# Six small changes of order in the two mixer layers and the second FFN of a fused transformer kernel on one Trainium2 core

## Chip, core, metric

The kernel runs on one core of one Trainium2 chip. Its engines are TensorE (PE in the profile: matmuls and transposes into PSUM), VectorE (DVE), ScalarE (ACT), GpSimd (POOL) and SyncE (SP, which issues the weight loads). Each engine executes its own list of instructions in order, and the lists meet only at semaphores. The metric is the device time of one execution in microseconds (us), lower is better; a comparison is made by the median of several runs.

## What is computed

The input is one sequence of 256 tokens of width 1024 in float32. Three blocks follow one another. The first has gated linear attention, sliding-window attention and a SwiGLU FFN ("f1"). The second and the third ("layer 0" and "layer 1") each mix with a latent attention and a gated recurrence (HGRN2), side by side:

```
proj = h @ w_in[l]          # split into c_q, c_kv, k_pe, hq, hf, hi, hg
q  = rmsnorm(c_q) @ w_q_b   ;  kv = rmsnorm(c_kv) @ w_kv_b        # "latents" c
a  = causal softmax attention of q against (k_nope, k_pe), 4 heads
f  = lb + (1 - lb) * sigmoid(hf);  k = (1 - lb) * sigmoid(-hf)    # lb: bounds of the layer
S_t = diag(f_t) S_{t-1} + k_t (x) hi_t ;  o_t = S_t^T silu(hq_t)
r  = rmsnorm(o) * silu(hg)
x  = x + concat(a, r) @ w_out[l]
```

The bounds `lb` come from a softmax over the two layers of `hg_lower_bounds`: zero in layer 0, one share per feature in layer 1. Layer 0 is followed by a SwiGLU FFN of inner width 2816 ("f2"), layer 1 by a mixture of 8 experts (top 2), and a last norm ends it.

## The kernel before

**Products.** Every float32 weight piece (128 partitions by 1024 values, two k-tiles of a 512-wide product) is split into a high part, rounded to fp32r, and a low part, the rest. ScalarE makes the high part (line 1542, `split_to`), and then GpSimd (line 669) or, inside the FFNs and the experts, VectorE (lines 2011, 1999) makes the low part by a subtract. TensorE forms three passes (lines 740 to 742): high by high, high by low, low by high. Four buffers hold pieces, so ScalarE may be four pieces ahead of TensorE (semaphore `w_used`). Products of 512 columns end in one of four "gemm banks" of PSUM, numbered by jobs (`gemm_at`); an engine that empties one counts `gemm_read`, and job j waits until job j-4 was read. The other four banks ("pair banks") take transposes and small products in the order of `pair_plan()`; TensorE counts `pair_full`, the reader `pair_read`, and a group waits until the bank's last user was read.

**Order.** Nothing is scheduled by a program: what each engine does and when is the order in which its block lists it. In TensorE's list (`gemm(..., between={...})`) small groups are put between the pieces of a large product.

**The mixers**, lines 1140 to 1290 (TensorE), 1720 to 1815 (ScalarE), 2375 to 2580 (VectorE). For the recurrence the 128 tokens of a tile are halved seven times ("levels", half sizes 64 to 1). Level n needs four steps of VectorE and two of ScalarE: `level_diff(n)` (lines 2439 and 2441, differences of summed log decays for keys and queries), `level_exp(n)` (1755, 1759), `level_scale(n)` (2450), TensorE's `level(n)` (1182, four head products), and `level_take(n)` (2464, masked copy into `n_at`). Level 0 is the diagonal. Other names that matter:

- `turn_gate` (1155 to 1165): waits for `n_lf_ready` (log decays) and forms their sums (1159), then for `n_k_ready` (log keys), transposes these (874), and forms the tails (1164).
- In layer 1, VectorE makes both (2394 to 2405): from `n_tmp[0]` (absolute value, then ScalarE's exponential, `z_odds`) `share` (2396), its product with `bound_rest`, two steps to `f_ready` (2399, 2400), `n_k` (2401), after ScalarE's logarithm `f_log` (1739) `n_lf` (2403), and with `log_rest` (ScalarE, 1735) the last of `n_k` (2405).
- `turn_c` transposes the latents `n_c` when `normalize_c` on VectorE (2493) is done; its factor is made on ScalarE by a logarithm and an exponential (1779, 1780), after the sums of squares (1774).
- `head_gemm` (836, 842): products of the latents with `qb0`, `qb1`, `kvb0`, `kvb1`.
- `hst` (1207): the state after the first tile, copied to `n_st` by VectorE in `copy_out` (1950). `mpT` (1216, 1220): rotated parts of queries and keys, transposed, copied by VectorE and read by the scores `msc0`, `msc1` (1232, 1236).
- `ho` (1247, 1250): output of the recurrence, copied by VectorE to `n_o`; ScalarE squares it (1804) for the norm. `mP` (1261): probabilities transposed; `mo` (1269): attention's output. `mixT` (1282): both transposed for `wo`, which starts in `first_mixed` (808).

TensorE's list from `hi` on is

```
gemm(hi, between={0: level(3), 2: turn_c})
qb0; level(4); qb1; kvb0; level(5); kvb1; hst; mpT; level(6); msc0; level(7); msc1; ho; mP; mo; mixT
```

and VectorE's, from taking level 3 on

```
take(3); cT copies; rotate k; scale(4); diff(5); gains; take(4); scale(5); diff(6); rotate q;
scale(6); take(5); diff(7); copy hst; copy mpT x2; scale(7); take(6); scores ...; copy ho x2; copy mP x3
```

**The FFN** "f2" runs in 11 units of 256 inner columns (`ffn`, lines 2296 to 2350 on VectorE; TensorE 1101 and 1104, `into_both`: all high products of a piece, then the low ones, which wait for VectorE's low half). Ahead of unit 3, VectorE does `finish_bounds()` (2288 to 2294): sum, reciprocal, product and one 1-wide step for layer 1's bounds.

Of the kernel before, what the change touches and what calls it, by code (L numbers as in the profile page):

```python
# [28 lines left out]
ALU = mybir.AluOpType  # L29
# [143 lines left out]
def pair_plan():  # L173

    plan = [("gT", 1), ("hT_f0", 4), ("z", 4), ("gb", 4), ("tail", 2), ("gkT", 2), ("gqT", 2), ("sT", 5),
            ("gsc", 4), ("ssc0", 4), ("gst", 4), ("ssc1", 4), ("go", 4), ("sP0", 4), ("sP1", 4), ("so", 4),
            ("posT", 1), ("soT", 4), ("goT", 4), ("mT", 4), ("hT_f1", 4), ("row_f1", 1)]
    for layer in range(2):
        level = [(f"hlev{n}_{layer}", 1 if n else T) for n in range(len(LEVELS) + 1)]
        plan += [(f"hT_l{layer}", 4), (f"msT_{layer}", 1), (f"hb_{layer}", 2), (f"hkT_{layer}", 2), (f"ht_{layer}", 1),  # L180
                 (f"hqT_{layer}", 2), *level[0:4], (f"cT_{layer}", 3), *level[4:6], (f"hst_{layer}", 1),
                 (f"mpT_{layer}", 2), level[6], (f"msc0_{layer}", 2),
                 level[7], (f"msc1_{layer}", 2), (f"ho_{layer}", 2), (f"mP_{layer}", 3), (f"mo_{layer}", 2),
                 (f"mixT_{layer}", 4),
                 (f"hT_g{layer}", 4)]
        if layer == 0:
            plan += [("row_g0", 1)]
    plan += [("router", 1), ("ranks", 1), ("counts", 1)]
    return plan


def build(nc, A, out):
    gemm_at, jobs = {}, 0
    for name, _, _, width, _ in gemm_plan():
# [78 lines left out]
    with ExitStack() as ctx:  # L273
# [463 lines left out]
        def _(pe):  # L737
# [410 lines left out]
            for l in range(2):  # L1148
# [45 lines left out]
                gemm(f"hi_{l}", between={0: lambda: level(3), 2: turn_c})  # L1194
# [9 lines left out]
                pe.wait_ge(sem("n_kt_ready"), l + 1)  # L1204
                b = pair(f"hst_{l}", 0)
                for i in range(HG_HEADS):
                    mm = pe.matmul(b[:, i * P:(i + 1) * P], n_kt[:, i * P:(i + 1) * P], n_v[:, 0, i * P:(i + 1) * P],
                                   start=True, stop=True)
                mm.then_inc(sem("pair_full"), 1)
# [33 lines left out]
                for t in range(T):  # L1243
                    b = pair(f"ho_{l}", t)
# [7 lines left out]
                    mm.then_inc(sem("pair_full"), 1)  # L1252
# [211 lines left out]
        def _(act):  # L1464
# [257 lines left out]
            for l in range(2):  # L1722
# [11 lines left out]
                if l == 1:  # L1734
                    act.activation(log_rest, bound_rest, ACT.Ln, bias=least_rest).then_inc(sem("rest_log"), 1)
# [36 lines left out]
                for t in range(T):  # L1772
# [6 lines left out]
                link(act.activation(head_rinv[:, 8:12], head_ms[:, 8:12], ACT.Ln))  # L1779
                act.activation(head_rinv[:, 8:12], head_rinv[:, 8:12], ACT.Exp, scale=-0.5) \  # L1780
                    .then_inc(sem("c_rinv"), 1)
# [18 lines left out]
                act.wait_ge(sem("pair_read"), pair_end[f"ho_{l}"])  # L1800
# [7 lines left out]
                act.activation(head_rinv[:, 0:8], head_ms[:, 0:8], ACT.Sqrt).then_inc(sem(f"head_root_{l}"), 1)  # L1808
                act.wait_ge(sem(f"head_root_{l}"), told(f"head_root_{l}"))
# [124 lines left out]
        def _(dve):  # L1934
# [353 lines left out]
            def finish_bounds():  # L2288

                dve.wait_ge(sem("bounds_exp"), 1)  # L2290
                link(dve.tensor_tensor(bound_sum, bound_rest, bound_low, ALU.add))
                link(dve.reciprocal(bound_sum, bound_sum))
                mul(bounds, bounds, over(bound_sum, 1, 2))
                link(dve.tensor_scalar(least_rest, ident[:, 0:1], 0.0, LEAST_REST, ALU.mult, ALU.add))
# [79 lines left out]
            for l in range(2):  # L2374
# [109 lines left out]
                def normalize_c():  # L2484
# [12 lines left out]
                def gate_hgrn():  # L2497

                    dve.wait_ge(sem(f"head_root_{l}"), 1)
# [20 lines left out]
                level_scale(3)  # L2520
                level_take(2)
# [12 lines left out]
                level_take(4)  # L2534
                level_scale(5)
# [6 lines left out]
                copy_out(f"hst_{l}", 0, n_st)  # L2542
# [19 lines left out]
                for t in range(T):  # L2562
                    copy_out(f"ho_{l}", t, n_o[:, t, :])

# [217 lines left out]
```

## Time and profile before

| | us |
|---|---|
| median of 3 runs | 1884.51 (1883.92 to 1885.49) |
| the profiled execution | 1884.52, its span 1882.6 |
| TensorE busy | 1859.7 (99%) |
| VectorE busy | 1520.7 (81%) |
| ScalarE busy | 1240.1 (66%) |
| GpSimd busy | 402.8 (21%) |
| chain that ended last | PE 90%, DVE 7%, ACT 1%, issue 1%, DMA 1% |

The span is the time from the first to the last instruction. In rows of the order of time, the first number is the start in us from the span's start, the second the duration (of x instructions together), and brackets hold the idle time before and what ended it. In rows of busy time by stretch, the columns are the stretch, its length, the busy time of PE, PEld (weight loads), DVE, ACT and POOL with their instructions, the granted clock of TensorE (1.00 is 2.4 GHz), the share of the DMA engines and GB/s. Layer 0's mixer lies at 455 to 600 us, the FFN f2 at 600 to 780, layer 1's mixer at 780 to 920, the experts after that. Matmuls are pipelined: a group's duration has a tail of about 0.2 us that the next group overlaps.

### The profile page before, as it was taken

Reading aid. Unit: us, or ns where it says so; the run is one execution under the profiler, and the core shown is the slowest. Engines: PE = TensorE matmul, PEld = TensorE weight load, DVE = VectorE, ACT = ScalarE, POOL = GpSimd, SP = SyncE. Lnnn points to the kernel's source line nnn. Section 1 sums busy time; section 2 is a strip of 40 time slices with the busy share of each in tenths; the row PEclk is TensorE's granted clock in tenths of the full one; section 3 lists DMA queues with packets and bytes.
Section 4 is the critical chain, followed back from the end, with each engine's and each line's share of the span. In section 5 each row is a group of like instructions: output and inputs, shape, how many; then the busy total and the mean of one; then the engine's idle time right before and its main releaser. Section 6 shows DMA issues by size and latency. Waiting matters only on the chain.

```text
span 1882.6 us, 26088 instructions
## 1 busy us (share of the span) xinstructions
PE 1859.7 (99%) x9336; PEld 1563.7 (83%) x9336; DVE 1520.7 (81%) x1650; ACT 1240.1 (66%) x1484; POOL 402.8 (21%) x206
## 2 busy tenths in 40 slices
PE   9999999999999999999999999999999999999997
PEld 7888889888888888878888888888888888888886
DVE  6745357777776887697699999999999999999997
ACT  6654444444754344565588888888888888888876
POOL 6856870002734000371630000000000000000000
PEclk9999999999999999999999999999999999999999
DMA  9534556665444666534699999999999999999994
GB/s 287 169 123 135 179 179 226 223 232 179 132 138 134 218 238 224 163 125 146 221 381 396 391 383 376 388 395 366 388 367 390 395 364 389 366 387 395 371 396 184
DMA packets 251542, 524.20 MB, mean 278 GB/s; under 512 B 9960, under 2 KB 58736, under 8 KB 251328
## 3 DMA queue, kind: packets, MB, share of 16 engines
q1 hardware_dynamic: 243408, 504.00, 74.7%
q10 hardware_dynamic: 5824, 12.06, 1.8%
q0 software_dynamic: 2224, 7.01, 1.2%
q8 instruction: 51, 0.84, 0.2%
q14 instruction: 35, 0.29, 0.0%
HBM read 507.71 MB, written 15.34 MB: 278 GB/s over the span
## 4 chain that ended last, share of the span: by engine, by line
PE 90%; DVE 7%; ACT 1%; issue 1%; DMA 1%; POOL 0%; SPq 0%; DVEq 0%; ACTq 0%
PE bank L740 24%; PE bank L742 24%; PE bank L741 24%; PE bank L1101 6%; PE bank L1104 3%; PE bank L863 1%; PE bank L1368 1%; PE bank L836 1%; DVE arena L1950 1%; DVE arena L2441 1%; DVE arena L1954 1%; PE bank L1182 1%; DMA arena<-in_w_in 1%; DVE arena L2106 1%; PE bank L842 0%
## 5 line engine op out<-in xcount | busy, mean ns | idle before, releaser
L1999 DVE TENSOR_TENSOR w_lo_sb<-arena,w_hi_sb 128x1024 fp32r<-128x1024 f32 x672 | 807.7, 1223 | 74.0 <-ACT w_hi_sb L1522 43.8
L1522 ACT ACTIVATE w_hi_sb<-arena 128x1024 fp32r<-128x1024 f32 x672 | 711.2, 1062 | 168.6 <-PE bank L742 167.9
L740 PE MATMUL bank<-w_hi_sb,left_sb 128*128 128x512 f32 (+1 forms) x1400 | 553.2, 395 | 1.4 <-POOL w_lo_sb L669 1.3
L742 PE MATMUL bank<-w_hi_sb,left_sb 128*128 128x512 f32 (+1 forms) x1400 | 542.2, 387 | 0.0
L741 PE MATMUL bank<-w_lo_sb,left_sb 128*128 128x512 f32 (+1 forms) x1400 | 541.5, 387 | 0.0
L1542 ACT ACTIVATE w_hi_sb<-arena 128x1024 fp32r<-128x1024 f32 (+1 forms) x269 | 278.2, 1051 | 300.8 <-PE bank L742 218.6
L669 POOL TENSOR_TENSOR w_lo_sb<-arena,w_hi_sb 128x1024 fp32r<-128x1024 f32 (+1 forms) x134 | 341.1, 2564 | 536.9 <-ACT w_hi_sb L1542 473.9
L740 PEld LDWEIGHTS bank<-w_hi_sb,left_sb 128*128 128x128 f32 x1400 | 263.1, 188 | 57.9 <-POOL w_lo_sb L669 3.5
L742 PEld LDWEIGHTS bank<-w_hi_sb,left_sb 128*128 128x128 f32 x1400 | 262.9, 188 | 54.9
L741 PEld LDWEIGHTS bank<-w_lo_sb,left_sb 128*128 128x128 f32 x1400 | 263.4, 188 | 50.9 <-issue 0.7
L740 PE MATMUL bank<-w_hi_sb,hid_hi_sb 128*128 128x512 f32 x656 | 257.3, 392 | 0.1
L741 PE MATMUL bank<-w_lo_sb,hid_hi_sb 128*128 128x512 f32 x656 | 255.6, 390 | 0.0
L742 PE MATMUL bank<-w_hi_sb,hid_lo_sb 128*128 128x512 f32 x656 | 255.4, 389 | 0.0
L2011 DVE TENSOR_TENSOR w_lo_sb<-arena,w_hi_sb 128x1024 fp32r<-128x1024 f32 x135 | 160.3, 1217 | 77.6 <-ACT w_hi_sb L1542 76.6
L724 POOL DMA_INDIRECT h_sb<-returned,arena x2 | 2.7, 1366 | 819.7 <-DMA returned<-arena 819.4
L742 PEld LDWEIGHTS bank<-w_hi_sb,hid_lo_sb 128*128 128x128 f32 x656 | 123.1, 188 | 25.9
L740 PEld LDWEIGHTS bank<-w_hi_sb,hid_hi_sb 128*128 128x128 f32 x656 | 123.3, 188 | 25.0 <-DVE w_lo_sb L1999 0.5
L741 PEld LDWEIGHTS bank<-w_lo_sb,hid_hi_sb 128*128 128x128 f32 x656 | 123.3, 188 | 24.2
L1101 PE MATMUL bank<-left_sb,w_hi_sb 128*128 128x512 f32 x512 | 127.8, 391 | 0.0
L1101 PEld LDWEIGHTS bank<-left_sb,w_hi_sb 128*128 128x128 f32 x512 | 93.1, 189 | 17.3
L1954 DVE TENSOR_TENSOR arena<-arena 128x512 f32<-128x512 f32 (+3 forms) x71 | 63.5, 894 | 23.1 <-ACT arena L1553 20.9
L1104 PEld LDWEIGHTS bank<-left_sb,w_lo_sb 128*128 128x128 f32 x512 | 69.8, 190 | 6.4 <-DVE w_lo_sb L2011 1.4
(365 smaller groups left out, 1676.1 us busy)
## 6 DMA issues: line engine op xcount, KB each, us to landing
arena<-in_moe_w_gate SPq DMA_DIRECT2D x112, 1024.0 KB, 7.6
arena<-in_moe_w_up SPq DMA_DIRECT2D x112, 1024.0 KB, 8.0
arena<-in_moe_w_down SPq DMA_DIRECT2D x112, 1024.0 KB, 7.8
arena<-in_w_in SPq DMA_DIRECT2D x45, 1024.0 KB, 5.1
arena<-in_w_ffn_in SPq DMA_DIRECT2D x22, 1024.0 KB, 5.1
arena<-in_w_out SPq DMA_DIRECT2D x12, 1024.0 KB, 5.0
arena<-in_w_ffn_out SPq DMA_DIRECT2D x11, 1024.0 KB, 4.8
arena<-in_dense_w_gate SPq DMA_DIRECT2D x11, 1024.0 KB, 5.4
```

Source lines behind the costliest of these rows:

```text
L669: pool.tensor_tensor(buffer(w_lo_sb, j, k, n), w, buffer(w_hi_sb, j, k, n).bitcast(F32), ALU.subtract).then_inc(sem("w_lo_by_gpsimd"), 1)
L740: pe.matmul(out, still[0], moving[0], start=start, stop=False)
L741: pe.matmul(out, still[0], moving[1], start=False, stop=False)
L742: return pe.matmul(out, still[1], moving[0], start=False, stop=stop)
L836: pe.matmul(gemm_bank[turned % 4][:, j * TOKENS:(j + 1) * TOKENS], w[:, k, j, 0:NOPE], n_cT[:, first + k, :], start=(k == 0), stop=(k == k ...
L1101: pe.matmul(sums, w_hi[:, k, :], left_both[:, :, k, :], start=(k == 0), stop=False)
L1104: mm = pe.matmul(sums[:, 0, :], w_lo[:, k, :], left_hi[:, k, :], start=False, stop=(k == KD - 1))
L1522: act.activation(expert_buffer(w_hi_sb, j), expert_piece(j % MOE_SUBS), ACT.Copy) \
L1542: act.activation(buffer(w_hi_sb, j, *w.shape[1:]), w, ACT.Copy).then_inc(sem("w_hi_ready"), 1)
L1954: dve.tensor_tensor(dst, one, two, ALU.mult).then_inc(sem(name), 1)
L1999: dve.tensor_tensor(expert_buffer(w_lo_sb, j), expert_piece(j % MOE_SUBS), expert_buffer(w_hi_sb, j).bitcast(F32), ALU.subtract) \
L2011: dve.tensor_tensor(buffer(w_lo_sb, j, *w.shape[1:]), w, buffer(w_hi_sb, j, *w.shape[1:]).bitcast(F32), ALU.subtract) \
```

## The change

Six edits, all in lists of order except that two make a factor in another way and one moves copies to another engine.

1. `finish_bounds(step)` is spread over units 3 to 6: sum and the 1-wide step, two halves of the reciprocal, the product.
2. In layer 1 ScalarE makes `log_rest` right after the norm's factor, before three weight casts; VectorE subtracts it from max(z, 0) as the first of its steps, and adds `soft` before `n_lf`.
3. TensorE does `level(3)` after the second piece of `hi` instead of after the first.
4. TensorE makes `hst` after `kvb0`, ahead of `level(5)`; VectorE copies it after `level_take(4)`, ahead of `level_scale(5)`; ahead of the `mpT` copies it waits for `level_diff(7)`.
5. The mean of the latents' squares is made before `level_take(2)`; ScalarE takes one square root and VectorE its reciprocal.
6. `ho` goes into gemm banks (two new jobs after `kvb1`); ScalarE copies it to `n_o`; VectorE's two copies go.

```
 pair_plan:
-    *level[0:4], (f"cT_{layer}", 3), *level[4:6], (f"hst_{layer}", 1), (f"mpT_{layer}", 2), level[6], ...
-    level[7], (f"msc1_{layer}", 2), (f"ho_{layer}", 2), (f"mP_{layer}", 3), (f"mo_{layer}", 2),
+    *level[0:4], (f"cT_{layer}", 3), level[4], (f"hst_{layer}", 1), level[5], (f"mpT_{layer}", 2), level[6], ...
+    level[7], (f"msc1_{layer}", 2), (f"mP_{layer}", 3), (f"mo_{layer}", 2),
 build:
+        if name.startswith("kvb1"):
+            gemm_at[name.replace("kvb1", "ho")], jobs = jobs, jobs + T
 TensorE:
-                gemm(f"hi_{l}", between={0: lambda: level(3), 2: turn_c})
+                gemm(f"hi_{l}", between={1: lambda: level(3), 2: turn_c})
...
                     head_gemm(f"kvb{i}_{l}", Q_RANK // P)
                     if i == 0:
+                        pe.wait_ge(sem("n_kt_ready"), l + 1)
+                        b = pair(f"hst_{l}", 0)
+                        (four head matmuls, then_inc pair_full)
                         level(5)
-                (the same five lines, after the loop)
...
                 for t in range(T):
-                    b = pair(f"ho_{l}", t)
+                    job = gemm_at[f"ho_{l}"] + t
+                    pe.wait_ge(sem("gemm_read"), job - 3)
+                    b = gemm_bank[job % 4]
...
-                    mm.then_inc(sem("pair_full"), 1)
+                    mm.then_inc(sem("ho_full"), 1)
 ScalarE:
                 if l == 0:
                     (bounds exponential)
+                else:
+                    act.activation(log_rest, bound_rest, ACT.Ln, bias=least_rest).then_inc(sem("rest_log"), 1)
                 split_to(span[f"hf_{l}"][1] + BUFFERS + 1)
                 (z_odds, z_soft)
-                if l == 1:
-                    act.activation(log_rest, bound_rest, ACT.Ln, bias=least_rest).then_inc(sem("rest_log"), 1)
...
-                link(act.activation(head_rinv[:, 8:12], head_ms[:, 8:12], ACT.Ln))
-                act.activation(head_rinv[:, 8:12], head_rinv[:, 8:12], ACT.Exp, scale=-0.5) \
-                    .then_inc(sem("c_rinv"), 1)
+                act.activation(head_rinv[:, 8:12], head_ms[:, 8:12], ACT.Sqrt).then_inc(sem("c_rinv"), 1)
...
-                act.wait_ge(sem("pair_read"), pair_end[f"ho_{l}"])
+                for t in range(T):
+                    act.wait_ge(sem("ho_full"), l * T + t + 1)
+                    act.activation(n_o[:, t, :], gemm_bank[(gemm_at[f"ho_{l}"] + t) % 4][:, :], ACT.Copy) \
+                        .then_inc(sem("gemm_read"), 1)
+                act.wait_ge(sem("gemm_read"), gemm_at[f"ho_{l}"] + T)
 VectorE:
+            def finish_bounds(step):
+                if step == 0:
+                    dve.wait_ge(sem("bounds_exp"), 1)
+                    link(dve.tensor_tensor(bound_sum, bound_rest, bound_low, ALU.add))
+                    link(dve.tensor_scalar(least_rest, ident[:, 0:1], 0.0, LEAST_REST, ALU.mult, ALU.add))
+                elif step <= 2:
+                    part = bound_sum[:, (step - 1) * 256:step * 256]
+                    link(dve.reciprocal(part, part))
+                else:
+                    mul(bounds, bounds, over(bound_sum, 1, 2))
...
-                    if tag == "f2" and u == 3:
-                        finish_bounds()
+                    if tag == "f2" and 3 <= u < 7:
+                        finish_bounds(u - 3)
...
                     odds, share = tiles(n_tmp[0]), tiles(n_tmp[2])
+                    dve.wait_ge(sem("rest_log"), 1)
+                    link(dve.scalar_tensor_tensor(n_k, n_z, 0.0, over(log_rest, 1, T), ALU.max, ALU.subtract))
                     dve.wait_ge(sem("z_odds"), 2)
                     (share, odds, then_inc f_ready)
-                    link(dve.scalar_tensor_tensor(n_k, n_z, 0.0, soft, ALU.max, ALU.add))
+                    dve.tensor_tensor(n_k, n_k, soft, ALU.add).then_inc(sem("n_k_ready"), 1)
                     dve.wait_ge(sem("f_log"), 1)
                     dve.tensor_tensor(n_lf, odds, soft, ALU.subtract).then_inc(sem("n_lf_ready_1"), 1)
-                    dve.wait_ge(sem("rest_log"), 1)
-                    dve.tensor_tensor(n_k, n_k, over(log_rest, 1, T), ALU.subtract).then_inc(sem("n_k_ready"), 1)
+                    dve.wait_ge(sem("n_k_ready"), 2)
...
+                def mean_c():
                     (the two means, out of normalize_c)
                 def normalize_c():
                     dve.wait_ge(sem("c_rinv"), l + 1)
+                    link(dve.reciprocal(head_rinv[:, 8:12], head_rinv[:, 8:12]))
...
                 level_scale(3)
+                mean_c()
                 level_take(2)
...
                 level_take(4)
+                copy_out(f"hst_{l}", 0, n_st)
                 level_scale(5)
...
                 level_diff(7)
-                copy_out(f"hst_{l}", 0, n_st)
+                dve.wait_ge(sem(f"level_diff_{l}"), 2 * len(LEVELS))
                 copy_out(f"mpT_{l}", 0, ...)
...
-                for t in range(T):
-                    copy_out(f"ho_{l}", t, n_o[:, t, :])
```

## Rows read from the trace of the kernel before

**Rows 1.** The page, part 1: busy time and share of the span by engine.

```profile
PE 1859.7 (99%) x9336; PEld 1563.7 (83%) x9336; DVE 1520.7 (81%) x1650; ACT 1240.1 (66%) x1484; POOL 402.8 (21%) x206
```

**Rows 2.** Order of time of TensorE, unit 3 of FFN f2.

```profile
647.05 1.22 PE L1104 MATMUL bank<-left_sb,w_lo_sb 128*128 128x256 f32 x8 [1.03 <-DVE w_lo_sb L2011]
```

**Rows 3.** Order of time of VectorE, unit 3 of FFN f2.

```profile
640.21 0.69 DVE L2291 TENSOR_TENSOR arena<-const_sb 128x512 f32<-128x512 f32 x1
640.94 3.35 DVE L2292 RECIPROCAL arena<-arena 128x512 f32<-128x512 f32 x1
...
645.77 4.63 DVE L2011 TENSOR_TENSOR w_lo_sb<-arena,w_hi_sb 128x1024 fp32r<-128x1024 f32 x4
```

**Rows 4.** Order of time of TensorE, layer 1's mixer.

```profile
809.29 2.05 PE L1159 MATMUL bank<-const_sb,arena 128*128 128x128 f32 x16 [0.45 <-DVE arena L2403]
812.61 1.09 PE L874 MATMUL bank<-const_sb,arena 128*128 128x128 f32 x8 [1.26 <-DVE arena L2405]
...
844.66 1.16 PE L1182 MATMUL bank<-arena 128*128 128x128 f32 x8 [1.16 <-DVE arena L2450]
```

**Rows 5.** Order of time of ScalarE, VectorE and GpSimd, start of layer 1's mixer.

```profile
790.62 1.06 ACT L1542 ACTIVATE w_hi_sb<-arena 128x1024 fp32r<-128x1024 f32 x1 [0.30 <-DVE small_sb L2032]
...
798.75 1.28 ACT L1733 ACT_TABLE_LOAD   x1
...
801.02 0.71 ACT L1735 ACTIVATE arena<-const_sb,small_sb 128x512 f32<-128x512 f32 x1
...
794.04 1.23 DVE L1966 SCALAR_TENSOR_TENSOR arena<-arena 128x1024 f32<-128x1024 f32 x1
798.85 2.12 DVE L2396 SCALAR_TENSOR_TENSOR arena<-arena 128x1024 f32<-128x1024 f32 x1 [3.58 <-ACT arena L1731]
...
803.52 3.29 DVE L2400 TENSOR_TENSOR arena<-arena 128x1024 f32<-128x1024 f32 x1
...
791.76 5.76 POOL L669 TENSOR_TENSOR w_lo_sb<-arena,w_hi_sb 128x1024 fp32r<-128x1024 f32 x2 [1.40 <-ACT w_hi_sb L1542]
794.11 3.41 POOL L669 TENSOR_TENSOR w_lo_sb<-arena,w_hi_sb 128x1024 fp32r<-128x1024 f32 x1
...
802.75 2.98 POOL L669 TENSOR_TENSOR w_lo_sb<-arena,w_hi_sb 128x1024 fp32r<-128x1024 f32 x1 [2.86 <-ACT w_hi_sb L1542]
```

**Rows 6.** Order of time of TensorE, middle of the mixers, last row layer 1.

```profile
544.66 1.05 PE L1182 MATMUL bank<-arena 128*128 128x128 f32 x8
545.55 1.89 PE L836 MATMUL bank<-arena 128*128 128x256 f32 x8
...
549.01 1.05 PE L1207 MATMUL bank<-arena 128*128 128x128 f32 x8
...
552.47 1.16 PE L1232 MATMUL bank<-arena 128*128 128x128 f32 x8 [0.86 <-DVE arena L1950]
...
875.23 1.16 PE L1232 MATMUL bank<-arena 128*128 128x128 f32 x8 [0.86 <-DVE arena L1950]
```

**Rows 7.** Busy time of each engine in a stretch; order of time of VectorE there.

```profile
538.91:552.43 13.52, 12.70 (x80) 11.55 (x78) 9.91 (x19) 6.20 (x11) 0.00 (x0) 1.00 0.73 261
...
542.37 1.08 DVE L1954 TENSOR_TENSOR arena<-arena,more_sb 128x256 f32<-128x256 f32 x3 [1.42 <-ACT arena L1562]
...
547.22 0.69 DVE L2450 TENSOR_TENSOR arena<-arena 128x512 f32<-128x512 f32 x1 [1.75 <-ACT arena L1759]
```

**Rows 8.** Order of time of VectorE, TensorE, ScalarE, end of layer 0's mixer.

```profile
560.94 3.58 DVE L1950 COPY arena<-bank 128x512 f32<-128x512 f32 x5
...
563.21 2.92 PE L1269 MATMUL bank<-arena 128*128 128x128 f32 x24 [0.36 <-DVE arena L1950]
...
564.44 0.29 ACT L1804 ACTIVATE arena<-arena 128x128 f32<-128x128 f32 x1
```

**Rows 9.** Busy time of each engine in two slices after the last matmul.

```profile
1875.00:1876.00 1.00, 0.00 (x0) 0.00 (x0) 0.74 (x2) 0.70 (x2) 0.00 (x0) 0.69 0.06 16
1876.00:1877.00 1.00, 0.00 (x0) 0.00 (x0) 0.71 (x1) 0.57 (x1) 0.00 (x0) 0.50 0.00 0
```

More of the change, by code:

```diff
@@ L180, in pair_plan @@
         plan += [(f"hT_l{layer}", 4), (f"msT_{layer}", 1), (f"hb_{layer}", 2), (f"hkT_{layer}", 2), (f"ht_{layer}", 1),
-                 (f"hqT_{layer}", 2), *level[0:4], (f"cT_{layer}", 3), *level[4:6], (f"hst_{layer}", 1),
+                 (f"hqT_{layer}", 2), *level[0:4], (f"cT_{layer}", 3), level[4], (f"hst_{layer}", 1), level[5],
                  (f"mpT_{layer}", 2), level[6], (f"msc0_{layer}", 2),
-                 level[7], (f"msc1_{layer}", 2), (f"ho_{layer}", 2), (f"mP_{layer}", 3), (f"mo_{layer}", 2),
+                 level[7], (f"msc1_{layer}", 2), (f"mP_{layer}", 3), (f"mo_{layer}", 2),
                  (f"mixT_{layer}", 4),
@@ L1202, in _ @@
                     if i == 0:
-                        level(5)
[L1204 to L1208, printed above, removed]
-                mm.then_inc(sem("pair_full"), 1)
+                        pe.wait_ge(sem("n_kt_ready"), l + 1)
+                        b = pair(f"hst_{l}", 0)
+                        for i in range(HG_HEADS):
+                            mm = pe.matmul(b[:, i * P:(i + 1) * P], n_kt[:, i * P:(i + 1) * P], n_v[:, 0, i * P:(i + 1) * P],
+                                           start=True, stop=True)
+                        mm.then_inc(sem("pair_full"), 1)
+                        level(5)
                 pe.wait_ge(sem(f"m_rot_{l}"), 2 * T)
@@ L1251, in _ @@
                                            n_st[:, i * P:(i + 1) * P], start=False, stop=True)
-                    mm.then_inc(sem("pair_full"), 1)
+                    mm.then_inc(sem("ho_full"), 1)
                 for t in range(T):
@@ L1807, in _ @@
                 act.wait_ge(sem(f"head_ms_h{l}"), 1)
-                act.activation(head_rinv[:, 0:8], head_ms[:, 0:8], ACT.Sqrt).then_inc(sem(f"head_root_{l}"), 1)
-                act.wait_ge(sem(f"head_root_{l}"), told(f"head_root_{l}"))
+                act.activation(head_rinv[:, 0:8], head_ms[:, 0:8], ACT.Sqrt).then_inc(sem("head_root"), 1)
+                act.wait_ge(sem("head_root"), told("head_root"))
                 if l == 1:
@@ L2286, in residual @@
                             mean_square("g1")
[L2288 to L2294, printed above, removed]
+            def finish_bounds(step):
[8 more added lines that the diff above has]
+                    mul(bounds, bounds, over(bound_sum, 1, 2))
             def ffn(tag, norm_tag, done, next_tag):
                 for u in range(FFN_UNITS):
-                    if tag == "f2" and u == 3:
-                        finish_bounds()
+                    if tag == "f2" and 3 <= u < 7:
+                        finish_bounds(u - 3)
                     gate_end, up_end = (span[f"{tag}_{kind}{u}"][1] for kind in ("gate", "up"))
@@ L2482, in rotate @@
                         dve.wait_ge(sem(f"m_rot_{l}"), told(f"m_rot_{l}"))
-                def normalize_c():
+                def mean_c():
                     dve.wait_ge(sem(f"c_ss_{l}"), 2 * T)
@@ L2488, in normalize_c @@
                     mean(head_ms[:, 10:12], head_ms[:, 10:12], KV_RANK, "c_ms")
+                def normalize_c():
                     dve.wait_ge(sem("c_rinv"), l + 1)
+                    link(dve.reciprocal(head_rinv[:, 8:12], head_rinv[:, 8:12]))
                     for n, (lo, hi) in enumerate(((0, Q_RANK), (Q_RANK, Q_RANK + KV_RANK))):
@@ L2497, in gate_hgrn @@
                 def gate_hgrn():
-                    dve.wait_ge(sem(f"head_root_{l}"), 1)
+                    dve.wait_ge(sem("head_root"), l + 1)
                     link(dve.reciprocal(head_rinv[:, 0:8], head_rinv[:, 0:8]))
```

## The prediction

> **What bounds the kernel now.** I read the page first: TensorE is busy for 99% of the span, VectorE for 81%, ScalarE for 66% [rows 1]. The time is therefore TensorE's work plus the places where it stands, and an edit counts only where it makes or removes such a place. The second view is TensorE's order of time in the stages that the edits touch. It shows four places where TensorE stands for VectorE: 1.03 us in the fourth unit of the second FFN (unit 3) for a weight piece's low half [rows 2]; in layer 1 0.45 us for the decay logarithms, 1.26 us for the keys `n_k` and 1.16 us for the third level's product [rows 4]; in layer 0 none of the last three. A fifth, 0.86 us ahead of the first scores, stands in layer 0 [rows 6] and likewise in layer 1. The third view is the order of time of VectorE, ScalarE and GpSimd ahead of each such place, for what is late there. After these stages come some 940 us of experts in which TensorE runs without a gap, so what is won or lost before them should reach the end unchanged (slices of the page: TensorE 9 throughout).
>
> The profiled execution took 1884.52 us (span 1882.6, 1.9 around it), and the median of the runs is 1884.51, so sums against the one hold for the other.
>
> **Bounds in four FFN units.** In unit 3 VectorE has 5.56 us of extra work (640.21 to 645.77), of which the 512-wide reciprocal is 3.35 [rows 3]. The low half that follows is ready late by the 1.03 us of TensorE's wait; with the restart after it, start to start, 1.2. So a unit hides 5.56 - 1.2 = 4.4 us of extra VectorE work. After the change the four units get at most: the sum and a 0.15 us scalar step (0.9 together), two halves of the reciprocal (about 1.7 each, half of 3.35), and the 1.23 us product. All lie under 4.4. **-1.2 us** (ends: -1.3 and 0, if another unit had no slack; TensorE has no other wait in the units that are built alike, so I take -1.2).
>
> **Early rest logarithm, layer 1.** ScalarE's `Ln` of 512 (0.71 us [rows 5]) moves ahead of three weight casts, and since the square root stands before it and an exponential after it, a table load of 1.28 us comes with it (such a one is in [rows 5]). The cast at 790.62 then starts about 1.9 us later, at 792.5, and GpSimd's low half of it at 793.6, where it started at 791.76. That matters through VectorE: a VectorE instruction with two operands in SBUF and a GpSimd one do not run side by side. The absolute value of 1.23 us (794.04) made a GpSimd subtract, 2.4 us when alone, last 3.41 us; `share` (L2396) took 2.12, and the sum L2400 3.29 us, beginning while GpSimd was in its piece of 802.75 to 805.73, and each ended about 1.1 us after GpSimd did [rows 5]. Whichever comes first holds the other up whole. So I let them take turns, 2.4 us against 1.1: GpSimd 793.6 to 796.0, absolute value to 797.1; GpSimd to 799.5, the new early `n_k` step to 800.6 (its logarithm has been ready since 792.4, so that wait is none); GpSimd to 803.0, `share` to 804.1; GpSimd (the fourth piece) to 806.5, the product with `bound_rest` to 807.6; then two steps alone to 810.1. Before, L2400 ended at 806.81. ScalarE's logarithm, the rest of `n_k` and `n_lf` follow as before, 2.5 us to TensorE's next group: 812.6 instead of 809.29. The keys are ready by then, so L874 follows L1159's sixteen directly (2.05 us, of which the next group overlaps some 0.2), at 814.4, where it stood at 812.61 [rows 4]. The removed wait of 1.26 comes back as a longer one of nearly 4 us. The other end: if the absolute value gets in ahead of GpSimd as now, L2400 ends where it did and the wait for the keys goes: -1.5 with its restart. +1.8 against -1.5; the row nearest to the new order (absolute value begins at 794.04, GpSimd's new start is 793.6) speaks for the loss; I take **+1.6**.
>
> The Trainium skill says it as a rule (SBUF — State Buffer, section "SBUF: two separate sides"): VectorE with two SBUF inputs and GpSimd take an exclusive lock on a shared port pair, and the later one blocks for the whole instruction. The trace agrees with its 2.12, 3.29 and 3.41 us. If the two shared bandwidth instead, the delay would be about half, and the sum some 1.6 us less.
>
> **Later third level, latents' factor by root.** Level 3 goes one piece of `hi` later, 2.7 us; the wait of 1.16 us in layer 1 [rows 4] is then covered, 1.3 with its restart, as long as VectorE's chain is late by less than that. The factor's chain is two table loads of 1.28 and two small steps (1.5 us each pair); one pair goes, and the mean is made before level 2 is taken, so the latents are normalized some 1.4 us earlier in layer 0, where TensorE did not wait for them: 0 there. The reciprocal adds 0.2 us on VectorE. In layer 1 VectorE is about 2.9 us late after the step above, TensorE 1.6, and the margin is used up: ends -1.5 and 0, I take **-1.3**, layer 1 alone.
>
> **Early state copy.** The diff does two things. TensorE makes the state `hst` after `kvb0` and before level 5. VectorE copies it right after it has taken level 4, ahead of scaling level 5. Times of layer 0: `kvb0` ends and the state can start at 544.66, where level 5 starts now, and the group takes 1.05 us (L1207) [rows 6]: 545.7. VectorE has taken level 4 by 538.9 and would stand for 6.9 us, where it now goes on with scale 5, difference 6, the rotation, scale 6, level 5, difference 7 and three copies. That stretch, 538.91 to 552.43, holds 13.52 us, of which 1.42 and 1.75 us are waits (for ScalarE, in turn for TensorE) [rows 7]: 10.35 us of chain. Begun at 545.8 (a signal costs about 0.1), it ends at 556.15 plus the new wait for difference 7, 0.1. The first scores start at 556.3 instead of 552.47 [rows 6]: **+3.8 us in each layer**; layer 1 has the same form (first scores at 875.23, after the same wait of 0.86). On the way TensorE stands about 1.7 us ahead of level 5 (state copy 0.69, scale 0.69, signals; it is free at 545.55) and about 3 us for the copies of `mpT`, since `kvb1` and the small groups fill only what lies between. What hung on the same VectorE steps moves with them: ScalarE's exponentials 6 and 7 wait for the differences, GpSimd's four pieces for scale 7; all keep their distance. Ends: -0.6 (VectorE is never held and its later copies are one shorter) and +4.0; the nearest rows are the measured chain, so +3.8. Two layers: **+7.6**.
>
> **Recurrent output to ScalarE.** VectorE's five copies of 3.58 us [rows 8] become three. TensorE's L1269 (0.36 us wait for them) can then start when its transposes are done, some 0.57 us earlier; the rest follows. ScalarE copies two banks (about 1.2 us) before its squares, whose last starts at 564.44 now and then at 565.6, while VectorE reads their sum after 566.4: hidden. If that cover is gone, it costs up to 0.7. The gemm banks used are free long before. **-1.1 us** in two layers (ends -1.4 and +0.3).
>
> **Sum.** -1.2 + 1.6 - 1.3 + 7.6 - 1.1 = +5.6: 1884.5 + 5.6 = **1890.1 us**. About 0.2% (3.8 us) is what a measurement of this kernel can tell from no change; the forecast is slower by 0.30%.
>
> **Rivals.**
> A. The state's wait holds, GpSimd and VectorE do not get in each other's way in layer 1. For: the order at 794 us hangs on 0.4 us. Then -1.2 - 1.5 - 1.6 + 7.6 - 1.1 = +2.2: 1886.7.
> B. TensorE's clock falls. The granted clock is 1.00 in all stages of these edits, but after the last matmul, at 1872.8, it went to 0.69 in the slice from 1875 and to 0.50 after that, 1.2 GHz [rows 9], so 2.5 us after the engine stopped. The new waits of 3 to 4 us are as long. No row shows TensorE working at half; the score groups and what follows to the outputs (552.47 to 560.9) hold some 5.6 us of matmuls that VectorE accompanies, so one fall costs between 0 and 5.6, nearer half: +2.4, 1892.5. Against: the waits lie between dense groups. The Trainium skill (TensorE: Matmul & The Clock Gate, section "Part 1: The HAM clock gate") says that activity releases a default half clock and idleness brings it back; the trace agrees with the fall.
> C. Faster: VectorE is not held at the state. Its place is 538.9 us; it decides if the state's bank is signalled before VectorE comes to it, 6.8 us sooner than by my reading of TensorE's order. Then -1.2 - 1.5 - 1.6 - 1.2 - 1.1 = -6.6: 1877.9. Against: the `hst` group stands behind three head products in TensorE's order.
> D. The hold is there but VectorE's chain shrinks by about half of it, as some of its instructions wait now for what will be long ready: +3.8 in both layers together, in all +1.8: 1886.3.
>
> **How the numbers follow.** Forecast 0.47 (own range 1888.5 to 1891.5), A 0.19, B 0.17, C 0.07, D 0.10. Faster by over 0.2%: C, 0.07 with a rest 0.08. Within: most of A and D, 0.24. Slower: forecast, B and the edge of A, 0.68. The range from 1886.2 to 1893.0 takes in A, B and D and leaves C out.
>
> **What would show it.** In the changed profile: VectorE's longest idle in each mixer is 6 to 7 us ahead of the copy of the state, released by TensorE; TensorE's L1182 (level 5) waits 1.5 to 2 us and its first score group 3 us for a copy; the first scores come 11.6 us after level 5's old place; the waits of unit 3, of `n_k` and of level 3 are gone; the wait for `n_lf` in layer 1 is about 4 us, and `share` takes over 3 us. Wrong would be: no idle at the state; `n_lf` at the old place; a granted clock below 1.00 in either mixer; or a total under 1886.

## The result, and the profile after

The changed kernel takes 1894.13 us in the median of six runs, the one before 1885.15 on the same chip: ratio 1.0048, 95% interval 1.0035 to 1.0061, so 9.0 us slower. The forecast was +5.6 (1890.1), the range ended at 1893.0: the direction was right, the size too small. The profiled execution of after took 1896.81 us, the slowest of the six (span 1894.1), 12.3 us above the traced execution of before; the table below says where. Three executions on record (one each of e4_only, e2_act and the kernel before) took over 3000 us, for no known reason, and the ratios leave them out.

TensorE is busy for 5.3 us more than before [rows 1], though it executes as many matmuls: the same instructions took longer.

```profile
PE 1865.0 (98%) x9336; PEld 1569.5 (83%) x9336; DVE 1522.3 (80%) x1649; ACT 1243.3 (66%) x1487; POOL 401.2 (21%) x206
```

TensorE in order of time, middle of layer 0's mixer, start of layer 1's, and the first scores of layer 1 [rows 4, 6]:

```profile
547.18 1.05 PE L1208 MATMUL bank<-arena 128*128 128x128 f32 x8
549.81 1.16 PE L1184 MATMUL bank<-arena 128*128 128x128 f32 x8 [1.58 <-DVE arena L2461]
...
558.78 2.07 PE L1234 MATMUL bank<-arena 128*128 128x128 f32 x8 [2.73 <-DVE arena L1956]
...
817.72 3.35 PE L1161 MATMUL bank<-const_sb,arena 128*128 128x128 f32 x16 [2.90 <-DVE arena L2415]
820.86 1.43 PE L876 MATMUL bank<-const_sb,arena 128*128 128x128 f32 x8
...
885.91 1.57 PE L1234 MATMUL bank<-arena 128*128 128x128 f32 x8 [2.73 <-DVE arena L1956]
```

The waits are at the places of the forecast: 1.58 us ahead of level 5, 2.73 ahead of the scores in both layers, 2.90 for `n_lf`. Read the second column too: the eight score matmuls (L1234) took 2.07 and 1.57 us where they took 1.16, and L1161's sixteen 3.35 where they took 2.05. Slices of the three places show why (last three columns: granted clock, DMA share, GB/s):

```profile
555.00:560.00 5.00, 2.27 (x15) 2.08 (x14) 4.83 (x8) 3.58 (x6) 0.47 (x1) 0.88 0.57 210
560.00:565.00 5.00, 5.00 (x30) 4.07 (x31) 3.68 (x7) 3.45 (x10) 5.00 (x3) 0.78 0.00 0
565.00:570.00 5.00, 4.76 (x40) 4.14 (x40) 3.30 (x5) 2.60 (x12) 3.86 (x2) 1.00 0.67 212
...
815.00:820.00 5.00, 2.28 (x12) 2.28 (x13) 3.20 (x4) 4.65 (x5) 2.57 (x2) 0.82 0.16 54
820.00:825.00 5.00, 5.00 (x25) 4.20 (x24) 3.18 (x6) 4.56 (x7) 5.00 (x3) 0.84 0.30 75
...
885.00:890.00 5.00, 4.09 (x23) 3.65 (x24) 4.09 (x8) 4.29 (x5) 3.34 (x2) 0.66 0.21 82
```

Granted clock 0.88 and 0.78 means that for (0.12 + 0.22) x 5 / 0.5 = 3.4 us of these ten the engine ran at the lower of its levels, 1.2 GHz. It did so while it worked again, after each wait of 2.7 to 2.9 us; behind the wait of 1.58 it kept 2.4 GHz (L1184 took 1.16). The Trainium skill (TensorE: Matmul & The Clock Gate, section "Part 1: The HAM clock gate") has the half clock come back with idleness; the trace agrees with its 2.07 for 1.16.

VectorE in order of time at the state's copy, which explains the first two waits [rows 7]:

```profile
540.69 0.73 DVE L2475 COPY_PREDICATED arena<-arena,bank 128x512 f32<-128x512 int32 x1
548.34 0.69 DVE L1956 COPY arena<-bank 128x512 f32<-128x512 f32 x1 [6.92 <-PE bank L1208]
...
557.57 1.15 DVE L1956 COPY arena<-bank 128x512 f32<-128x512 f32 x2
```

It stands for 6.92 us, and what follows, 548.34 to 558.72 (10.38 us), is the chain that the forecast took as 10.35. Next, ScalarE, GpSimd and VectorE at the start of layer 1's mixer [rows 5] (all 5.9 us later than before by what lies ahead):

```profile
796.23 1.28 ACT L1734 ACT_TABLE_LOAD   x1
797.52 0.72 ACT L1734 ACTIVATE arena<-const_sb,small_sb 128x512 f32<-128x512 f32 x1
798.15 1.99 ACT L1546 ACTIVATE w_hi_sb<-arena 128x1024 fp32r<-128x1024 f32 x2
...
799.27 12.44 POOL L671 TENSOR_TENSOR w_lo_sb<-arena,w_hi_sb 128x1024 fp32r<-128x1024 f32 x4 [3.02 <-ACT w_hi_sb L1546]
...
799.93 2.83 DVE L1972 SCALAR_TENSOR_TENSOR arena<-arena 128x1024 f32<-128x1024 f32 x1
802.80 3.31 DVE L2406 SCALAR_TENSOR_TENSOR arena<-arena 128x1024 f32<-128x1024 f32 x1
806.14 3.32 DVE L2408 SCALAR_TENSOR_TENSOR arena<-arena 128x1024 f32<-128x1024 f32 x1
809.50 3.30 DVE L1960 TENSOR_TENSOR arena<-arena,const_sb 128x1024 f32<-128x1024 f32 x1
812.83 1.23 DVE L2411 SCALAR_TENSOR_TENSOR arena<-arena,const_sb 128x1024 f32<-128x1024 f32 x1
```

Four GpSimd pieces stand beside four VectorE operations; the latter end 2.8 to 3.3 us after they began, the fifth, alone again, after 1.23. That is the turn-taking of the forecast.

**A table of stages.** Executions reach layer 0's mixer up to 3.6 us apart (TensorE's L863 there starts between 456.5 and 460.2), though no edit touches what lies ahead. So I cut every trace at the same eight instructions of TensorE and compare the pieces. The differences in us to the kernel before: (1) start of layer 0's mixer to its first scores, (2) on to the output projection L808, (3) on to L885 behind the second FFN, (4) on to layer 1's turn L1159, (5) on to its query products L836, (6) on to its scores, (7) on to L808.

| kernel | 1 | 2 | 3 | 4 | 5 | 6 | 7 |
|---|---|---|---|---|---|---|---|
| before (us) | 94.82 | 15.88 | 221.01 | 19.93 | 45.93 | 20.01 | 15.88 |
| after | +3.80 | +0.92 | -1.34 | +2.54 | -1.54 | +3.79 | +0.92 |
| e4_only | +3.75 | +1.49 | -0.07 | 0.00 | -0.03 | +3.78 | +1.40 |
| e4_behind5 | +4.23 | +0.01 | -0.04 | +0.01 | +0.01 | +3.06 | +1.52 |
| filled | +3.75 | -0.59 | -1.31 | +2.55 | -3.13 | +3.79 | -0.61 |
| all_but_4 | -0.04 | -0.58 | -1.31 | +2.54 | -1.52 | +0.01 | -0.59 |
| e126 | -0.04 | -0.60 | -1.36 | +2.52 | -1.10 | 0.00 | -0.59 |
| e2_only | +1.17 | +0.02 | 0.00 | +2.54 | -1.50 | 0.00 | +0.01 |
| e2_act | -0.02 | +0.01 | -0.04 | +1.36 | -0.01 | 0.00 | +0.01 |
| e1356 | -0.05 | -0.58 | -1.33 | 0.00 | -1.71 | 0.00 | -0.59 |
| mid_copy | -0.60 | +0.09 | -1.29 | +0.01 | -1.71 | -0.61 | +0.09 |
| e2_f2 | +1.12 | -0.58 | -0.61 | +0.92 | -3.16 | -0.01 | -0.59 |
| combo | +0.56 | +0.10 | -0.57 | +0.93 | -3.13 | -0.61 | +0.09 |

The rest, from L808 to the end, is 991.5 us in the kernel before and within 0.3 of it in all of them. The line of after adds to +9.1; its traced execution also came 2.5 us later to the first stage.

Two things in these traces come from no edit. The first lies ahead of the stages: in after TensorE waited 2.26 us for GpSimd in the first block and the clock fell behind that wait too, and likewise in e1356 behind 1.85 us. These are the two executions that came latest to layer 0 (460.2 and 459.9). After's row and its slice:

```profile
46.74 0.75 PE L742 MATMUL bank<-w_hi_sb,left_sb 128*128 128x512 f32 x1 [2.26 <-POOL w_lo_sb L671]
...
45.00:50.00 5.00, 3.26 (x8) 2.58 (x9) 4.86 (x5) 4.94 (x7) 5.00 (x3) 0.68 0.10 37
```

The second is the 1.06 us that stage 1 holds too much in e2_only, e2_f2, combo and e4_behind5. A VectorE step of two columns (L1958), 0.2 us at most in the other nine traces, began there 0.01 to 0.02 us behind a GpSimd subtract and took 2.4 us; TensorE waited 0.91 us for it. VectorE and GpSimd in e2_only, and in before:

```profile
468.69 2.39 DVE L1958 TENSOR_SCALAR small_sb<-small_sb 128x2 f32<-128x2 f32 x1
468.68 2.37 POOL L669 TENSOR_TENSOR w_lo_sb<-arena,w_hi_sb 128x1024 fp32r<-128x1024 f32 x1 [0.51 <-ACT w_hi_sb L1542]
```

```profile
468.21 0.17 DVE L1958 TENSOR_SCALAR small_sb<-small_sb 128x2 f32<-128x2 f32 x1
468.21 2.42 POOL L669 TENSOR_TENSOR w_lo_sb<-arena,w_hi_sb 128x1024 fp32r<-128x1024 f32 x1 [0.51 <-ACT w_hi_sb L1542]
```

### The profile page after: what moved, and what is told of

Same layout as the page of the kernel before. It is cut to its first block, busy times and chain, and to the rows that moved or that the text cites. A ratio compares the mean times of both kernels' runs of the same rounds, so it can differ in the third digit from the quotient of the medians.

```text
span 1894.1 us, 26089 instructions
## 1 busy us (share of the span) xinstructions
PE 1865.0 (98%) x9336; PEld 1569.5 (83%) x9336; DVE 1522.3 (80%) x1649; ACT 1243.3 (66%) x1487; POOL 401.2 (21%) x206
## 4 chain that ended last, share of the span: by engine, by line
PE 94%; DVE 3%; DMA 1%; issue 1%; ACT 1%; POOL 0%; SPq 0%; DVEq 0%; ACTq 0%; POOLq 0%
PE bank L742 25%; PE bank L744 25%; PE bank L743 25%; PE bank L1103 6%; PE bank L1106 3%; PE bank L865 1%; PE bank L1372 1%; PE bank L838 1%; PE bank L1184 1%; PE bank L844 1%; DMA const_sb<-in_const_table 1%; DMA arena<-in_w_in 1%; PE bank L1012 0%; PE bank L1234 0%; PE bank L989 0%
```

## The experiments

Each was run with the kernel before on the same chip; edits are numbered 1 bounds, 2 early rest logarithm, 3 later level 3, 4 early state copy, 5 latents' factor by root, 6 recurrent output to ScalarE.

**e4_only, edit 4 alone** (its lines of the diff, nothing else).

> The kernel before with edit 4 alone (the recurrent state made ahead of level 5 and copied by VectorE ahead of level 5's operand). Theory 1: VectorE is held 6.9 us ahead of the copy in each layer, TensorE waits twice behind it (+3.8 us a layer), and in the second wait the granted clock falls (some +1.5 us a layer): +9 to +11 us against before, level 5 entered after a wait of 1.6 us, the scores after one of 2.7 us, granted clock under 0.9 in the 5 us behind the scores' start. Theory 2 (the hold costs its waits and no more; the rest of the loss is that of the early logarithm): +7.6 us. Theory 3 (most of the 9 us is not edit 4's): +4 us or less.

Measured: 1896.32 (1896.15 without the long one) against 1885.39, ratio 1.0053 [1.0040, 1.0066]. Theory 1 holds in every part: stages 1 and 6 each +3.8, stages 2 and 7 +1.5 and +1.4. TensorE of this kernel:

```profile
548.08 1.16 PE L1182 MATMUL bank<-arena 128*128 128x128 f32 x8 [1.58 <-DVE arena L2450]
...
557.04 2.07 PE L1232 MATMUL bank<-arena 128*128 128x128 f32 x8 [2.73 <-DVE arena L1950]
```

**e2_only, edit 2 alone.**

> The kernel before with edit 2 alone (the rest logarithm of the bounds ahead of the odds' exponential in layer 1, its subtraction at the front of VectorE's work). Theory 1: VectorE's operations on the gates come beside GpSimd's low halves and both take turns, so n_lf comes later and TensorE waits 2.9 us for it instead of 2.05: +1.6 us, and +2.5 to +3 if the granted clock falls in that wait. Theory 2 (the removed operation behind the f logarithm was worth more): -1.3 us. Both leave layer 0 as it was.

Measured: 1886.27, ratio 1.0005 [0.9996, 1.0014], +0.9 and within the noise, between the numbers of the two theories. (The 2.05 of the expectation is the length of L1159's group; its wait was 0.45.) The wait for `n_lf` grew to 2.95, as theory 1 has it, and the clock fell (0.91 and 0.75 in the slices from 810 and 815), yet stages 4 and 5 add to only +1.04. The run e126 below shows why.

**all_but_4, all edits but 4.**

> The changed kernel without edit 4. Theory 1 (edit 4 carries +9 to +11): -2 to 0 us against before, no wait ahead of level 5, scores' wait at 0.86 us as before. Theory 3 (the others carry the loss): +5 us or more.

Measured: 1883.94, ratio 0.9988 [0.9979, 0.9997], -1.45. Theory 1: without edit 4 the rest of the change gains a little, though the clock fell behind the turn's wait of 2.95 us here too. With e4_only it shows that edit 4 makes the change slow.

**e1356, the changed kernel without 2 and 4.**

> The changed kernel without edits 2 and 4. Theory 1: the remaining four edits save what the forecast gave them, -1.2 (bounds) -1.3 (level 3 and the latents' root, layer 1) -1.1 (recurrent output to ScalarE) = -3.6 us, with no new clock fall. Theory 3 (the small gains are hidden or given back): 0 to -1 us.

Measured: 1882.13, ratio 0.9978 [0.9969, 0.9988], so -3.3 in the median; by stages -1.33, -1.71 and twice -0.59, -4.2. The two numbers differ by less than the spread of its own runs (1879.27 to 1882.93). Together these four edits do what the forecast gave them.

**filled, the clock by itself.** Matmuls whose operands (whatever `hid_lo_sb` holds) and results nobody uses, in the three waits:

```
                     if i == 0:
                         ...
+                        pe.wait_ge(sem("gemm_read"), gemm_at[f"kvb1_{l}"] - 3)
+                        keep_clock(6, gemm_bank[(gemm_at[f"kvb1_{l}"]) % 4])
                         level(5)
...
                 level(6)
+                pe.wait_ge(sem("gemm_read"), gemm_at[f"ho_{l}"] - 3)
+                keep_clock(11, gemm_bank[gemm_at[f"ho_{l}"] % 4])
                 pe.wait_ge(sem("pair_read"), pair_end[f"mpT_{l}"])
...
                 def turn_gate():
+                    if l == 1:
+                        keep_clock(11, pair(f"hb_{l}", 0))
                     pe.wait_ge(sem(f"n_lf_ready_{l}"), 1)
```

> The changed kernel with idle matmuls (operands and results nobody uses) put into TensorE's three long waits: 6 ahead of level 5 and 11 ahead of the first scores in each layer, 11 ahead of the gate's turn in layer 1. The waits stay as long as they were, only TensorE works in them. Theory 1 (the fallen clock behind the waits costs 1.5 us per layer at the scores and 1.6 us at layer 1's turn): 4.6 us less than the changed kernel, so +4.4 us against before, L1232's first scores and the turn take 1.16 and 2.05 us again. Theory 2 (the clock is not what costs; the rest of the loss sits elsewhere): +9 us as the changed kernel, or more by the matmuls that outlast the waits.

Measured: 1890.63 against 1885.09, ratio 1.0030 [1.0018, 1.0042], +5.5 where the changed kernel had +9.0. The intervals of the two ratios overlap a little; the trace is what decides. TensorE, L893 being the added matmuls, and a slice behind them:

```profile
554.17 2.77 PE L893 MATMUL bank<-hid_lo_sb 128*128 128x512 f32 x11
557.16 1.16 PE L1240 MATMUL bank<-arena 128*128 128x128 f32 x8 [0.22 <-DVE arena L1962]
...
811.54 2.65 PE L893 MATMUL bank<-hid_lo_sb 128*128 128x512 f32 x11
814.63 2.05 PE L1163 MATMUL bank<-const_sb,arena 128*128 128x128 f32 x16 [0.44 <-DVE arena L2421]
...
560.00:565.00 5.00, 5.00 (x36) 4.14 (x36) 4.11 (x7) 2.80 (x12) 5.00 (x4) 1.00 0.23 47
```

Stages 1, 4 and 6 are what they are in after, to 0.05: the scores and the turn come no earlier. What follows them is faster by 1.51, 1.59 and 1.53: 4.6 us in all, and groups take 1.16 and 2.05 again. With only these matmuls added, that is the clock's price in the traced execution. The medians differ by 3.4 us, not 4.6; the last part says why.

**e4_behind5, where the hold acts.** Edit 4 with the copy one step later:

```
                 level_take(4)
-                copy_out(f"hst_{l}", 0, n_st)
                 level_scale(5)
+                copy_out(f"hst_{l}", 0, n_st)
```

> The kernel before with edit 4, but VectorE copies the state behind level 5's operand instead of ahead of it. Theory 1 (VectorE's held chain, not TensorE's wait at level 5, sets the scores): the wait of 1.58 us ahead of level 5 goes, the one ahead of the scores grows by about as much, and the scores come only 0.72 us earlier in each layer than with edit 4, the length of the operand that no longer follows the copy: some 1.4 us less than edit 4 alone (+10.9), so about +9 to +9.5 us against before. Rival (the two waits of TensorE add up, each with its own price): 3.2 us less than edit 4 alone, +7.7 us.

Measured: 1892.81 against 1885.0, ratio 1.0040 [1.0027, 1.0054]: +7.8, the rival's number, though the interval takes in theory 1's +9. The trace speaks for theory 1 all the same. TensorE:

```profile
546.25 1.06 PE L1182 MATMUL bank<-arena 128*128 128x128 f32 x8
...
551.61 0.66 PE L1216 MATMUL bank<-const_sb,arena 128*128 128x128 f32 x4 [0.85 <-DVE arena L2477]
...
556.23 1.16 PE L1232 MATMUL bank<-arena 128*128 128x128 f32 x8 [2.73 <-DVE arena L1950]
...
882.04 1.92 PE L1232 MATMUL bank<-arena 128*128 128x128 f32 x8 [2.73 <-DVE arena L1950]
```

Level 5's wait is gone, and layer 1's scores come +3.06 late instead of +3.78: 0.72 less, not 1.6. The rest of the gain is one clock fall that didn't happen: after 2.73 us of standing, layer 0's scores took 1.16 and layer 1's, after the same 2.73, 1.92. I had expected the scores' wait to grow; the wait went to L1216 instead, for the rotation. (Stage 1 shows +4.23 here, with the 1.06 us of L1958; from `kvb0` on, 541.91 to 556.23, it is 14.32 against 15.05 in e4_only, again 0.73 less.)

**e2_act, ScalarE's half of edit 2.**

```
                     act.activation(bounds, bounds, ACT.Exp).then_inc(sem("bounds_exp"), 1)
+                else:
+                    act.activation(log_rest, bound_rest, ACT.Ln, bias=least_rest).then_inc(sem("rest_log"), 1)
...
-                if l == 1:
-                    act.activation(log_rest, bound_rest, ACT.Ln, bias=least_rest).then_inc(sem("rest_log"), 1)
```

> The kernel before with ScalarE's part of edit 2 alone: the rest logarithm and its table load come ahead of the cast at 790.62 us, VectorE's order is as before. Theory 1 (the delayed cast moves GpSimd's low half beside VectorE's gate work, and both take turns): the turn's wait grows nearly as with the whole of edit 2, from 0.45 to some 2.5 to 3 us, +1.0 to +2.3 us against before. Rival (it is VectorE's new operation at the front that stands beside GpSimd): no change, 0 to +0.3 us.

Measured: 1886.14, ratio 1.0005 [0.9996, 1.0015], within the noise; stage 4 shows +1.36, in theory 1's range, with a wait of 1.77 us and not 2.5 to 3. TensorE, VectorE and GpSimd:

```profile
810.46 2.05 PE L1159 MATMUL bank<-const_sb,arena 128*128 128x128 f32 x16 [1.77 <-DVE arena L2403]
...
793.85 2.84 DVE L1966 SCALAR_TENSOR_TENSOR arena<-arena 128x1024 f32<-128x1024 f32 x1
...
793.20 12.45 POOL L669 TENSOR_TENSOR w_lo_sb<-arena,w_hi_sb 128x1024 fp32r<-128x1024 f32 x4 [3.02 <-ACT w_hi_sb L1542]
```

GpSimd begins at 793.20, ahead of the absolute value, as reckoned (793.6). It makes about half of the loss of 2.54; the rest goes with VectorE's added operation, one more turn (0.92 by itself in e2_f2, the next run).

**e2_f2, the logarithm where ScalarE has room.** Edits 1, 3, 5, 6 and VectorE's order of edit 2, with

```
                         .then_inc(sem(f"{tag}_silu"), 1)
+                    if tag == "f2" and u == FFN_UNITS - 1:
+                        act.activation(log_rest, bound_rest, ACT.Ln, bias=least_rest).then_inc(sem("rest_log"), 1)
```

> Edits 1, 3, 5 and 6, and edit 2 with VectorE's new order, but the rest logarithm taken in the last unit of the second layer's feed-forward part, on ScalarE behind its Silu. Theory 1 (edit 2 lost by its delayed cast): the cast at 790.62 is not delayed, VectorE has one operation less behind the f logarithm, the wait of 1.26 us for n_k goes: 1.2 us less than the four edits, some -4.5 us against before. Rival (VectorE's operation at the front stands beside GpSimd's low half wherever the logarithm is made): the turn's wait stays at some 3 us and the clock falls, +2 us against the four edits, so -1.3 us.

Measured: 1881.27 against 1885.09, ratio 0.9981 [0.9972, 0.9990]: as e1356, between the two theories. VectorE and TensorE:

```profile
794.19 1.22 DVE L1972 SCALAR_TENSOR_TENSOR arena<-arena 128x1024 f32<-128x1024 f32 x1
795.45 3.31 DVE L2406 SCALAR_TENSOR_TENSOR arena<-arena 128x1024 f32<-128x1024 f32 x1
...
810.36 2.05 PE L1161 MATMUL bank<-const_sb,arena 128*128 128x128 f32 x16 [1.41 <-DVE arena L2415]
```

The absolute value is undisturbed at 1.22, but the new operation costs its turn (3.31): stage 4 +0.92. Stage 5 wins 1.45 over e1356 (the keys' wait is gone), and stage 3 loses 0.72 at the end of the FFN, which neither theory had (combo, with the same logarithm, loses as much): nothing is left.

**e126, edits 1, 2 and 6.**

> Edits 1, 2 and 6. With edit 2 in place level 3's wait of 1.16 us is gone of itself, since the turn ahead of it comes later. Theory (edit 2 and the later level 3 remove the same wait, so 3 and 5 are worth nothing beside edit 2): as the changed kernel without edit 4, -1.2 us against before. Rival (the edits add up): 1.7 us slower than that, +0.5 us.

Measured: 1885.37 against 1885.00, ratio 0.9999 [0.9990, 1.0009], +0.4. That is near the rival's +0.5, but the interval takes in both numbers, and the stages add to -1.2; what decides is stage 5. TensorE of this kernel, and under it the turn in e2_only:

```profile
810.76 2.05 PE L1161 MATMUL bank<-const_sb,arena 128*128 128x128 f32 x16 [2.92 <-DVE arena L2417]
...
845.02 1.16 PE L1184 MATMUL bank<-arena 128*128 128x128 f32 x8 [1.57 <-DVE arena L2463]
```

```profile
813.50 3.31 PE L1159 MATMUL bank<-const_sb,arena 128*128 128x128 f32 x16 [2.95 <-DVE arena L2405]
```

Here the clock held after 2.92 us, and level 3 waited 1.57; in e2_only it fell after 2.95, and level 3 didn't wait at all. So stage 5 has four values: without 3 and 5, -1.10 (clock held) and -1.50 (fell); with them, -3.13 (filled, held) and -1.52 (all_but_4, fell). A fallen clock costs 1.6 us where nothing stands behind it, and nothing where TensorE would have waited for VectorE anyway. Edits 3 and 5 save 1.7 alone and some 2.0 beside edit 2, or nothing when the clock falls. So each theory holds for one case: the first where the clock falls, the rival where it doesn't.

**mid_copy, a better place for the state.** Edits 1, 3, 5, 6, TensorE's order of edit 4, and in VectorE's:

```
                 rotate(lambda t: n_pq[:, t, :].rearrange("p (h d) -> p h d", h=MLA_HEADS), MLA_HEADS)
+                copy_out(f"hst_{l}", 0, n_st)
                 level_scale(6)
```

> Edits 1, 3, 5 and 6, and edit 4 in TensorE's order alone (the state ahead of level 5), while VectorE copies it behind the rotation, where it stood idle for 1.75 us (ahead of its row at 547.22). Theory 1: VectorE's copy is not held and is no longer between level 5's take and the copies that the first scores wait for, so these come 0.62 us earlier in each layer: 1.2 us less than the four edits alone, some -4.5 us against before. Rival (the state product ahead of level 5 costs TensorE as much as it gives VectorE, or the copy delays level 6's operand): as the four edits, -3.3 us, or worse.

Measured: 1880.97 against 1885.09, ratio 0.9978 [0.9969, 0.9987]: as the four edits. TensorE and VectorE:

```profile
552.13 1.16 PE L1234 MATMUL bank<-arena 128*128 128x128 f32 x8 [0.25 <-DVE arena L1956]
...
555.49 1.97 PE L1234 MATMUL bank<-arena 128*128 128x256 f32 x8 [0.47 <-DVE h_sb L2570]
...
546.09 0.69 DVE L1956 COPY arena<-bank 128x512 f32<-128x512 f32 x1 [0.35 <-PE bank L1208]
...
552.79 0.69 DVE L2460 TENSOR_TENSOR arena<-arena 128x512 f32<-128x512 f32 x1 [0.72 <-ACT arena L1763]
```

The copy waits 0.35 us instead of 6.92, and the scores come 0.6 earlier as foreseen. But VectorE then waits 0.72 (not at all in e1356) for ScalarE's exponential of level 7, and TensorE's second score group 0.47 for a bank: stages 2 and 7 give the 0.6 back.

**combo**, mid_copy with the logarithm of e2_f2.

> Edits 1, 3, 5 and 6, with the state copy behind the rotation and the rest logarithm in the feed-forward part. Each gave -0.5 us at most over the four edits alone: -3.3 to -4.5 us against before.

Measured: 1881.46 against 1885.00, ratio 0.9979 [0.9970, 0.9988]. Both kernels, before and after, are beaten by e1356, mid_copy, e2_f2 and combo, whose medians can't be told apart.

## Why the prediction was wrong, point by point

- **Bounds**: -1.2 forecast, -1.3 measured (stage 3). Right.
- **Early state copy**: +3.8 a layer, +3.80 and +3.79 measured; idle 6.92 of 6.9, level 5's wait 1.58 of "1.5 to 2", the scores' 2.73 of "about 3". Right, and rivals C and D fell: VectorE is held, and its chain didn't shrink.
- **Recurrent output**: -1.1 forecast, -0.59 twice. Right.
- **Early rest logarithm**: the mechanism was right. The wait came out at 2.90, not "nearly 4", and the turn +2.55, not +3.3: its turns were counted 0.7 us too long. Rival A (no conflict) fell.
- **Later level 3 and the root**: -1.3 forecast, -1.71 alone. Stages 4 and 5 with the clock held (filled) give 2.55 - 3.13 = -0.6 for edits 2, 3 and 5, against +0.3 forecast.
- **The step that failed is the sum's treatment of the clock**, which it put at nothing. The forecast had it in rival B, at 0.17 and as one fall of 0 to 5.6, "nearer half: +2.4", against which stood that "the waits lie between dense groups". Its own waits of about 3 us stood in three places, and in the profiled execution the clock fell in all three, which the prediction itself had named as a sign of being wrong. Each fall cost 1.5 to 1.6, so 4.6 in all. That sum would have been 5.6 + 4.6 = 10.2, less 0.9 for the last two points and 0.2 for small ones: 9.1, as the stages of that execution add to. The filled kernel is the forecast's case, and took +5.5 in the median, +4.5 by its stages.
- **That 9.1 meets the median's +9.0 so closely is partly chance.** The other five executions of after have no trace. Their mean granted clocks are 0.995 to 0.997, the traced one's 0.994 and the kernel before's 0.998 or 0.999; one fall of 3.4 us lowers the mean by 0.0009, so most of them seem to have had fewer falls than the traced one's four, of which one lies in the first block (an estimate). Fewer than three falls in the stages, on average, also fits the 3.4 us that the filling won in the medians.
- **A slip without weight**: rivals A and C take the later level 3 at -1.6, past the end of -1.5 that its own term gives.

What remains open is why the clock fell in one place and not in the next after waits of one length: 2.73 us, layers 0 and 1 of e4_behind5; 2.92 and 2.95 us, e126 and e2_only. It changes from execution to execution of one kernel: of e126's eleven, four show a mean clock of 0.997, where the traced one without a fall shows 0.999.

## What to carry to other kernels

When a copy is moved ahead in an in-order engine, look up when its producer is made before you count what it frees: 0.7 us of copy held VectorE for 6.9. A wait that you forecast on TensorE is to be priced with the clock behind it, here 2.7 to 2.9 us of standing and up to 1.6 more at half speed, once per place, and not in every execution. And read a gain at the next wait, not where it is made: twice (mid_copy, e2_only) a later wait gave back or took up what an earlier place had won or lost.

## What the runs showed of the hardware

- The granted clock fell behind eight of the ten unfilled waits of 2.7 to 2.95 us in the traces of after, e4_only, e4_behind5, e2_only, all_but_4 and e126, and behind none of the eight of 1.4 to 1.8 us in the mixers. It also fell behind the 2.26 and the 1.85 us in the first block of after and e1356. Unused matmuls in the three waits kept it at 1.00.
- GpSimd's subtract and VectorE's operations of two SBUF operands take turns over a whole row of them: four VectorE operations of 1.23 us alone took 12.8 us beside four GpSimd ones, 2.4 each when alone. The Trainium skill (SBUF — State Buffer, section "SBUF: two separate sides") tells of one holding the shared ports for a whole instruction; the trace agrees, 2.83 to 3.32 us each.
- Which of the two is held up can hang on 0.01 us: a VectorE step of two columns took 0.17 us when it began together with GpSimd's subtract or ahead of it (468.21 and 468.21), and 2.4 us when it began 0.01 to 0.02 us behind (468.69 and 468.68). That moved TensorE by 1.06 us, as much as single edits here do.
- Thirteen traces reached layer 0's mixer up to 3.6 us apart through the same instructions; a wait on GpSimd with a clock fall behind it made the two latest. Pieces between fixed instructions that no edit and no such event touched agreed to 0.1 us.
